# Resting tiles of 96 columns instead of 128 in the expert stage of a two-layer encoder kernel

## The reference

```
logits = (h @ router); top_v, top_i = lax.top_k(logits, 2)
top_w = softmax(top_v); comb = sum(one_hot(top_i, 8) * top_w[..., None], axis=-2)
out = 0
for e in range(8):
    out += comb[..., e:e+1] * ((silu(h @ wg[e]) * (h @ wu[e])) @ wd[e])
```

## Time and profile before

| what | us |
|---|---|
| median of 3 runs | 1901.2 |
| lowest and highest | 1900.38, 1902.32 |
| profiled execution: span from first to last instruction | 1901.2 |
| TensorE busy in it | 1863.4 (98%) |
| VectorE, ScalarE, GpSimd busy | 1442.3, 1166.7, 173.3 |

### The profile page before, as it was taken

One profiled execution on the slowest core, in us unless ns is written; L12 is line 12 of the kernel. 1 busy time (PEld: TensorE's weight loads), 2 busy tenths in 40 slices (PEclk: granted clock), 3 DMA queues, 4 the chain that ended last, 5 costly groups with the idle time before them and its releaser, 6 DMA issues.

```text
span 1901.2 us, 26671 instructions
## 1 busy us (share of the span) xinstructions
PE 1863.4 (98%) x10298; PEld 1508.3 (79%) x10298; DVE 1442.3 (76%) x1487; ACT 1166.7 (61%) x1153; POOL 173.3 (9%) x164
## 2 busy tenths in 40 slices
PE   7999999999999999999999999999999999999998
PEld 6878766788888787667888888888888888888886
DVE  4678575544546785755998989989888888898897
ACT  4575324543544663244777777777777777777776
POOL 1263003100001630031000000000000000000000
PEclk9999999999999999998999999999999999999999
DMA  9642223653556332224999999999999999999995
GB/s 313 203 156 104 90 90 133 211 193 137 199 196 214 131 131 90 90 89 146 359 361 343 367 347 358 370 341 358 365 346 365 348 356 362 341 366 347 359 367 219
DMA packets 182541, 487.79 MB, mean 257 GB/s; under 512 B 5896, under 2 KB 12676, under 8 KB 173640
## 3 DMA queue, kind: packets, MB, share of 16 engines
q1 hardware_dynamic: 177296, 477.50, 68.9%
q0 software_dynamic: 1488, 5.57, 0.9%
q10 hardware_dynamic: 3688, 3.74, 0.7%
HBM read 482.03 MB, written 1.05 MB: 254 GB/s over the span
## 4 chain that ended last, share of the span: by engine, by line
PE 88%; DVE 7%; ACT 2%; DMA 2%; issue 1%; POOL 0%; SPq 0%; DVEq 0%; ACTq 0%
PE bank L1848 48%; PE bank L1245 26%; PE bank L1458 2%; PE bank L1797 2%; PE bank L1429 1%; PE bank L1859 1%; DMA ring<-w_o_dram 1%; PE bank L1817 1%; DVE y_rwkv L1916 1%; PE bank L1237 1%; DVE ring_lo L1916 1%; DVE tmp L1916 1%; DMA h<-x_dram 1%; DVE gT_lo L1916 0%; DMA ring<-w_in_dram 0%
## 5 line engine op out<-in xcount | busy, mean ns | idle before, releaser
L1916 DVE TENSOR_TENSOR w_lo<-ring,w_hi 128x2048 fp32r<-128x2048 f32 x337 | 767.3, 2289 | 112.5 <-ACT w_hi L1147 104.1
L1147 ACT ACTIVATE w_hi<-ring 128x2048 fp32r<-128x2048 f32 x320 | 612.2, 1916 | 122.8 <-PE bank L1848 110.0
L1848 PE MATMUL bank<-w_hi,xg_hi 128*128 128x512 f32 x896 | 354.4, 396 | 1.1 <-DVE w_lo L1916 1.1
L1848 PE MATMUL bank<-w_hi,xg_lo 128*128 128x512 f32 x896 | 349.7, 390 | 0.0
L1848 PE MATMUL bank<-w_lo,xg_hi 128*128 128x512 f32 x896 | 349.5, 390 | 0.0
L1848 PEld LDWEIGHTS bank<-w_hi,xg_hi 128*128 128x128 f32 x896 | 168.8, 188 | 38.1 <-DVE w_lo L1916 4.3
L1848 PEld LDWEIGHTS bank<-w_hi,xg_lo 128*128 128x128 f32 x896 | 168.2, 188 | 35.5
L1848 PEld LDWEIGHTS bank<-w_lo,xg_hi 128*128 128x128 f32 x896 | 168.3, 188 | 33.9 <-issue 0.2
L1848 PE MATMUL bank<-w_hi,ehT_hi 128*128 128x512 f32 x448 | 176.5, 394 | 0.0
L1848 PE MATMUL bank<-w_hi,ehT_lo 128*128 128x512 f32 x448 | 174.8, 390 | 0.0
L1848 PE MATMUL bank<-w_lo,ehT_hi 128*128 128x512 f32 x448 | 174.5, 390 | 0.0
(11 more groups left out here) (434 smaller groups left out, 3036.4 us busy)
## 6 DMA issues: line engine op xcount, KB each, us to landing
ring<-moe_w_gate_dram SPq DMA_DIRECT2D x57, 2048.0 KB, 7.8
ring<-moe_w_up_dram SPq DMA_DIRECT2D x56, 2048.0 KB, 8.3
ring<-moe_w_down_dram SPq DMA_DIRECT2D x56, 2048.0 KB, 9.6
ring<-w_in_dram SPq DMA_DIRECT2D x26, 2048.0 KB, 8.1
ring<-w_branch_dram SPq DMA_DIRECT2D x6, 2048.0 KB, 8.3
ring<-ffn_w_gate_dram SPq DMA_DIRECT2D x5, 2048.0 KB, 8.1
ring<-ffn_w_up_dram SPq DMA_DIRECT2D x5, 2048.0 KB, 8.0
ring<-ffn_w_down_dram SPq DMA_DIRECT2D x5, 2048.0 KB, 8.3
```

What stands on the lines that cost most here:

```text
L1147: A.activation(w_hi[:, q % PARTS, :], ring[:, i, o:o + HALF], ACT.Copy).then_inc(s.hi_ready, 1)
L1848: ins = M(dst, a, w, start=start and n == 0, stop=stop and n == 2, skip_group_check=True)
L1916: return V.tensor_tensor(out_, a, b, op)
```

## The change

An item holds 96 slots instead of 128 (`CAP`). The resting tiles are 128 rows x 96 columns, the outputs of the large products lie on 96 partitions, an item's tokens take 96 columns of a bank; the gather streams 96 columns of `sel`; the transposes in `turn` read 96 rows of `ehm` and stream a 96x96 identity; scatter sums over 96 rows. An expert may now need up to three items and the list has room for five further ones, so `spos` and `comb` have three groups, and the list's arithmetic is written anew. The table of constants is 16 columns (64 bytes a partition) longer.

```
+CAP = 96
+GROUPS = -(-SEQ // CAP)
+MORE = (SEQ * 2 - NE) // CAP
-    c["slots"] = np.tile(np.arange(P, dtype=np.float64), (P, 1))
+    c["slots"] = np.tile(np.where(i < CAP, i, 0.5), (P, 1))
+    c["later"] = np.tile(2 * NE - np.arange(2 * NE, dtype=np.float64), (P, 1))
-    xg_hi = sb("xg_hi", [P, KD, P], F32R, where=X + 49152)
-    ehT_hi = sb("ehT_hi", [P, 28, P], F32R, where=X + 57344)
+    xg_hi = sb("xg_hi", [P, KD, CAP], F32R, where=X + 49152)
+    ehT_hi = sb("ehT_hi", [P, 28, CAP], F32R, where=X + 57344)
...
-                        ins = M(b[:, i * P:(i + 1) * P], hn[:, t, n * P:n * P + P], sel[:, t, :], start=t == 0,
+                        ins = M(b[:, i * CAP:(i + 1) * CAP], hn[:, t, n * P:n * P + P], sel[:, t, 0:CAP], start=t == 0,
...
-                        ins = M(b[:], selT[:, t * P:(t + 1) * P], part[:, 512 * u:512 * u + 512], start=i == 0,
+                        ins = M(b[:], selT[0:CAP, t * P:(t + 1) * P], part[0:CAP, 512 * u:512 * u + 512], start=i == 0,
...
-                    ins = TR(b[:, c * P:(c + 1) * P], ehm[:, j % 2, c:512:4], ident)
+                    ins = TR(b[:, c * CAP:(c + 1) * CAP], ehm[0:CAP, j % 2, c:512:4], ident[0:CAP, 0:CAP])
...
-                            ins = three(b[:], xg_hi[:, x, :], xg_lo[:, x, :], q % PARTS,
+                            ins = three(b[0:CAP, :], xg_hi[:, x, :], xg_lo[:, x, :], q % PARTS,
...
-                            ins = TR(b[:, t * P:(t + 1) * P], sel[:, t, :], ident)
+                            ins = TR(b[0:CAP, t * P:(t + 1) * P], sel[:, t, 0:CAP], ident)
...
-                            ins = three(b[:], ehT_hi[:, x, :], ehT_lo[:, x, :], q % PARTS,
+                            ins = three(b[0:CAP, :], ehT_hi[:, x, :], ehT_lo[:, x, :], q % PARTS,
...
-        for i in range(2):
-            step(V.tensor_scalar(spos[:, i, :, :], R(5), -1.0 - P * i, None, ALU.add))
+        for i in range(GROUPS):
+            step(V.tensor_scalar(spos[:, i, :, :], R(5), -1.0 - CAP * i, None, ALU.add))
-        free(V.tensor_scalar(f[:, 0:8], b[0:1, 16:24], P + 0.5, None, ALU.is_gt), "rank.1")
+        step(V.tensor_scalar(f[:, 0:8], b[0:1, 16:24], CAP + 0.5, None, ALU.is_gt))
+        free(V.tensor_scalar(f[:, 8:16], b[0:1, 16:24], 2 * CAP + 0.5, None, ALU.is_gt), "rank.1")
...
-                tt(ey_lo[:, cols], b[:], ey_hi[:, cols].bitcast(F32), ALU.subtract).then_inc(s.freed_vec, 1)
+                tt(ey_lo[0:CAP, cols], b[0:CAP, :], ey_hi[0:CAP, cols].bitcast(F32), ALU.subtract)\
+                    .then_inc(s.freed_vec, 1)
...
-                    tt(ehT_lo[:, 4 * j:4 * j + 4, :], b[:].rearrange("p (c n) -> p c n", c=4),
+                    tt(ehT_lo[:, 4 * j:4 * j + 4, :], b[:, 0:4 * CAP].rearrange("p (c n) -> p c n", c=4),
```

More of the change, by code:

```diff
@@ L480, in build @@
     rt = sb("rt", [P, 16, T, NE], where=X + 101376)
-    it_f = sb("it_f", [1, 64], where=X + 102656)
+    it_f = sb("it_f", [1, 96], where=X + 113664)
     items = sb("items", [1, 32], I32, where=X + 102912)
-    spos = sb("spos", [P, 2, T, NE], where=X + 103040)
-    comb = sb("comb", [P, 2, T, NE], where=X + 103168)
+    spos = sb("spos", [P, GROUPS, T, NE], where=X + 103040)
+    comb = sb("comb", [P, GROUPS, T, NE], where=X + 103232)
     higher = sb("higher", [P, T, NE, NE], where=X + 112640)
@@ L682, in _ @@
         sp.wait_ge(s.items_ready, 1)
-        n_items = sp.value_load(items[0:1, 24:25], min_val=SURE, max_val=SURE + 3)
+        n_items = sp.value_load(items[0:1, 26:27], min_val=SURE, max_val=SURE + MORE)
         with sp.If(n_items > SURE):
             with sp.Fori(SURE, n_items) as item:
-                e = sp.value_load(items[0:1, bass.ds(item + 12, 1)], min_val=0, max_val=NE - 1)
+                e = sp.value_load(items[0:1, bass.ds(item + NE + MORE, 1)], min_val=0, max_val=NE - 1)
                 expert_panels(e, item)
@@ L1118, in gathered_hi @@
                 for i in range(4):
-                    ins = A.activation(xg_hi[:, 4 * u + i, :], b[:, i * P:(i + 1) * P], ACT.Copy,
+                    ins = A.activation(xg_hi[:, 4 * u + i, :], b[:, i * CAP:(i + 1) * CAP], ACT.Copy,
                                        scale=gains[:, 1, 1, 4 * u + i:4 * u + i + 1])
@@ L1130, in _ @@
         act.wait_ge(s.items_ready, 1)
-        n_items = act.value_load(items[0:1, 24:25], min_val=SURE, max_val=SURE + 3)
+        n_items = act.value_load(items[0:1, 26:27], min_val=SURE, max_val=SURE + MORE)
         with act.Fori(0, n_items) as item:
@@ L1807, in _ @@
         pe.wait_ge(s.items_ready, 1)
-        n_items = pe.value_load(items[0:1, 24:25], min_val=SURE, max_val=SURE + 3)
+        n_items = pe.value_load(items[0:1, 26:27], min_val=SURE, max_val=SURE + MORE)
         def scatter(item, b_of):
@@ L2460, in _ @@
         settle()
-        step(V.tensor_scalar(selT[:], cst[:, 0:SEQ], 0.0, None, ALU.mult))
+        step(V.tensor_scalar(selT[0:CAP, :], cst[0:CAP, 0:SEQ], 0.0, None, ALU.mult))
         step(V.memset(weight[:], 0.0))
         select(0)
-        step(V.tensor_scalar(f[:, 8:16], C("experts")[0:1, :], -1.0, 8.0, ALU.mult, ALU.add))
+        more = slice(0, MORE)
+        over, first, upper = f[:, 24:32][:, more], f[:, 32:40][:, more], f[:, 40:48][:, more]
+        step(tt(f[:, 64:80], C("later")[0:1, :], f[:, 0:16], ALU.mult))
@@ L2466, in _ @@
+        step(V.reduce_sum(f[:, 56 + 26:56 + 27], f[:, 0:16], AX.X))
         settle()
-        step(tt(f[:, 8:16], f[:, 8:16], f[:, 0:8], ALU.mult))
-        step(V.reduce_sum(f[:, 56:57], f[:, 0:8], AX.X))
+        step(V.max(f[:, 16:24], f[:, 64:80]))
         settle()
-        step(V.max(f[:, 16:24], f[:, 8:16]))
+        step(V.tensor_scalar(over, f[:, 16:24][:, more], -1.0, 2.0 * NE, ALU.mult, ALU.add))
+        step(V.tensor_scalar(f[:, 82:83], f[:, 82:83], float(NE), None, ALU.add))
         settle()
-        step(V.tensor_scalar(f[:, 40:44], f[:, 16:20], -1.0, 24.0, ALU.mult, ALU.add))
@@ L2473, in _ @@
[L2473 to L2476, removed]
+        step(V.tensor_scalar(over, over, 2.0 * NE - 1, None, ALU.min))
         settle()
-        step(V.tensor_scalar(f[:, 52:56], f[:, 52:56], float(NE - 1), None, ALU.min))
-        step(V.tensor_scalar(f[:, 40:44], f[:, 40:44], float(2 * NE * T // 2 + NE - 1), None, ALU.min))
+        step(V.tensor_scalar(upper, over, NE - 0.5, float(NE), ALU.is_gt, ALU.mult))
@@ L2480, in _ @@
         settle()
-        step(V.tensor_copy(items[0:1, 0:25], f[:, 32:57]), s.items_ready)
+        step(tt(first, over, upper, ALU.add))
+        step(tt(over, over, upper, ALU.subtract))
+        settle()
+        step(V.tensor_scalar(f[:, 56 + NE:56 + NE + MORE], first, float(NE * T), None, ALU.add))
+        step(V.tensor_copy(f[:, 56 + 2 * NE + MORE:56 + 2 * NE + 2 * MORE], over))
+        step(V.tensor_copy(f[:, 56:56 + NE], C("experts")[0:1, :]))
+        step(V.tensor_copy(f[:, 56 + NE + MORE:56 + 2 * NE + MORE], C("experts")[0:1, :]))
@@ L2482, in _ @@
+        settle()
+        step(V.tensor_copy(items[0:1, 0:27], f[:, 56:83]), s.items_ready)
         dve.wait_ge(s.route_exp, 1)
@@ L2504, in gathered_lo @@
                     c = 4 * u + i
-                    ins = V.scalar_tensor_tensor(out=xg_lo[:, c, :], in0=b[:, i * P:(i + 1) * P],
+                    ins = V.scalar_tensor_tensor(out=xg_lo[:, c, :], in0=b[:, i * CAP:(i + 1) * CAP],
                                                  scalar=gains[:, 1, 1, c:c + 1], in1=xg_hi[:, c, :].bitcast(F32),
@@ L2525, in _ @@
         gathered_lo(lambda job: ahead(dve, job), 0)
-        n_items = dve.value_load(items[0:1, 24:25], min_val=SURE, max_val=SURE + 3)
+        n_items = dve.value_load(items[0:1, 26:27], min_val=SURE, max_val=SURE + MORE)
         with dve.Fori(0, n_items) as item:
-            next_column = dve.value_load(items[0:1, bass.ds(item + 1, 1)], min_val=0, max_val=NE * T + NE - 1)
+            next_column = dve.value_load(items[0:1, bass.ds(item + 1, 1)], min_val=0, max_val=NE * T * (GROUPS - 1) + NE - 1)
             def item_product(job):
```

16 lines of the change are left out of this document (8 added, 8 removed).

## The result

The changed kernel takes 1913.22 us (1912.49 to 1913.90, four runs), the kernel before 1901.43 (1900.38 to 1902.32, four runs). The ratio is 1.0068, with a 95% interval of 1.0056 to 1.0080: slower by 0.7%. The profiled execution has a span of 1910.8 us against 1901.2.

A forecast was written before the change was run, and what follows sets the result against it. TensorE's time per instruction was taken to bound the expert stage. Terms of 0 and -0.2 us summed to -0.2 us against the 1901.2 us span; likeliest time 1901.0 us, range 1887 to 1908.

The forecast's parts named there:

- second rival: Large products slow because pace depends on operand places; up to 233.4 ns each, 26 us more, 1927 us; chance 0.14.
- first rival: Large products' extra time belongs to the weight load, a quarter goes: 13.7 us less, 1887.5 us; chance 0.21.
- The large products, entered at 0: 504 an item, 4032 in all: shortening their hidden weight load changes nothing; entered 0, lower bound by the line -1.4 us.
- The gather: 32 instructions an item: the load of 128 columns sets the rate, so 0; other bound 8.0 us less.
- The turns: Seven an item: the stepped load of 128 columns sets the rate, so 0; other bound 6.6 us less.
- Scatter and the transposes of the selection: Scatter still streams 512 columns past 128 resting; the two `sel` transposes still stream 128: 0 for both.
- VectorE and ScalarE: In the loop they read a quarter fewer columns under a TensorE that doesn't wait for them: 0.
- The routing: Once: VectorE's added list operations, 0.5 to 1 us, fit into 2.74 us idle; smaller tiles after the gather save 0.1 to 0.2.
- The third: Gather and turns go with the streamed columns: 14.6 us less, 1886.6 us; chance 0.05.
- the fifth: The change runs a ninth item: 2025 us; chance 0.01.
- The fourth: Loads of 96 columns lose a fast path that 128 has: some 390 us more, 2290 us; chance 0.01.
- The limit on any gain: DMA would bind next at about 118.8 us an item, so the expert stage could give at most 40 us, 1861.

The follow-up runs named there:

- e16: Kernel before, only the large products resting on 96 columns and writing 96 partitions, step still 512 bytes; 1911.76 us against 1900.35, ratio 1.0059.
- e15: Kernel before, with padding so that streamed and resting tiles of all stages lie multiples of 256 bytes apart; 1890.41 us against 1900.35, ratio 0.9950.
- e5: Kernel before, large products reading their 128 resting columns 128 bytes behind a tile's start; 1922.16 us against 1901.03, ratio 1.0101.
- e13: Kernel before, resting tiles and all behind them moved by 128 bytes, streamed halves left in place; 1917.25 us, ratio 1.0084.
- e2: Changed kernel with tiles of 128 columns at a step of 512 bytes, list still for items of 96; 1899.75 us, ratio 0.9991.
- e1: Changed kernel, its 96-column resting tiles beginning every 512 bytes instead of every 384; 1907.11 us against 1900.42, ratio 1.0030.
- e3: Kernel before, large products reading resting tiles of 128 columns at a step of 384 bytes, overlapping; 1917.28 us against 1900.42, ratio 1.0080.
- e14: Kernel before, only the large products resting on 64 columns and writing 64 partitions; 1909.09 us against 1900.35, ratio 1.0048.
- e12: Kernel before, streamed and resting tiles of the expert stage moved together by 128 bytes; 1901.07 us, ratio 1.0003.
- e6: Changed kernel with 80 columns a tile at a step of 512 bytes; 1916.52 us against 1901.03, ratio 1.0080.

## Why the prediction was wrong

The forecast was 1901.0 us and no change, with 1887 to 1908 as the range. The measured 1913.22 lies above it, on the side of the second rival, which had a chance of 0.14: a pace that depends on where the operands lie. Its sign, more than 30.1 us for the piece of 132, came up with 30.60. That rival named one of two causes and was too large in price: I priced it with the dense part's 233.4 ns, 26 us. The piece of 132 shows 231.8 ns, and over its 504 products an item grew by 116.84 - 114.91 = 1.93 us, 15.4 us for eight. The other cause, that a narrower tile is slower by itself, stood in no rival; the first one had the width, with the opposite sign.

*The items, the bound, the load.* Right: eight items, TensorE alone in the chain before and after, and loads of 161 ns as the line between 134 and 188 gave.

*The large products, entered at 0.* This is the step that failed, in two places. The first is the sentence that shortening a hidden thing gives nothing. It was used as if it also meant that it costs nothing. e16 changes the width of the large products alone, and they take 116.02 us an item instead of 114.91; the kernel loses 0.59%. The second is the reading of the earlier trace rows. I took the extra of 20.1 ns at 512 and 10.7 ns at 256 columns for a cost that goes with the streamed columns. In both rows some distances were no multiple of 256 bytes: by the layout the streamed `f_hi` and the resting `fx_lo` lie at 96 bytes beyond a multiple of 256, the streamed `ring_lo` and the resting `fx_hi` at 128. Lined up, in e15, the extra is 227.3 - 213.3 = 14.0 ns at 512 columns and 119.9 - 106.7 = 13.2 ns at 256: nearly the same for both, as a cost per load would be. So the places added 6.1 ns at 512 columns and took 2.5 ns off at 256, and that, not the streamed columns, had made the extra seem to halve. Even so, the first rival's conclusion didn't follow: the extra is per product, and fewer resting columns made it larger, not smaller.

*The waits.* The prediction says that no row of the view of the earlier trace rows has TensorE waiting. That view was cut to its longest rows. Over the whole expert stage, from 900 to 1901 us, there is one (us in total, times, longest us):

```profile
PEld bank L1848 <- DVE w_lo L1916: 4.3, 10, 1.5
```

From 1000 to 1850 us it is 2.5 us, 0.3% of that time, so the conclusion, that TensorE's own time counts, stands.

*The second rival's evidence.* I counted it against the rival that `xg` and `ehT` lie at different places and have one pace. They do, but their places differ by multiples of 512 bytes, so they were the same place by the rule that e5 to e13 found. The evidence for it, one instruction with two paces in one trace, was the better of the two, and the two changes of address that I named (384 bytes, 64 bytes) should have been checked each for what it does to the distance between the operands. The 64 bytes moved streamed and resting tiles of the expert stage together (e2: nothing); the 384 bytes did not.

*How the loss splits.* The starts of the pieces of 132 give the length of an item: 123.80 us before, 124.92 in e16 (1249.43 to 1374.35), 124.68 in e1 (1243.85 to 1368.53), 125.55 in the changed kernel. Taken in this order, the width costs 1.12 us an item, the shorter turns and gather give 0.24 back, and the step of 384 bytes costs 0.87: 8 x (1.12 - 0.24 + 0.87) = 14.0 us. But the two causes don't add. With 128 columns the same step alone makes an item 125.79 us (e3), 1.99 over before, and its 132 products take 30.59 us where the changed kernel's take 30.60: at this step the narrower tile costs nothing more. So the loss has no split that is independent of the order.

*The gather.* Right: 3.54 us for 3.57. Streaming 96 instead of 128 columns past 128 resting ones hardly changes the pace, which fits a pace set by the load. *The turns.* Entered at 0, with 6.6 us as the other bound; they fell from 0.47 to 0.445 us, 56 x 0.025 = 1.4 us. *Scatter and the transposes of the selection.* 1.84 for 1.82 and 0.22 for 0.22.

*VectorE and ScalarE.* Right: 0.9 us less an item on VectorE, worth nothing. *The routing.* Right in that it stayed covered, and right in price: from the start of the second `sel` to the end of the small copy VectorE took 3.11 us before and 3.61 us after, 0.5 us more. The cover was less than I gave. VectorE was idle for 0.29 us ahead of the first `xg_lo`, not 2.74. The 2.74 came from the lower clock in that execution, which delayed the gather; in most of the executions with the old list, e5 for one, the same wait was 1.07 us or 1.06. So the longer list used up most of what cover there was.

```profile
890.86 0.16 DVE L2508 COPY smax<-smax 128x2 f32<-128x2 f32 x1
891.30 0.99 DVE L2516 SCALAR_TENSOR_TENSOR xg_lo<-bank,gains,xg_hi 128x96 fp32r<-128x96 f32 x4 [0.29 <-ACT xg_hi L1123]
```

*The other rivals.* The third fell with the gather, the fifth with the count of items. The fourth, the loss of a fast load, is refuted: the loads of the large products take 135 ns for 64 columns (e14), 161 for 96 and 188 for 128, about 0.83 ns a column throughout, so 128 columns have no fast path that 96 could lose. The rule of the Trainium skill that stood behind it ("TensorE: Matmul & The Clock Gate", section Weight-path perf modes), by which four-byte types gain nothing from it, agrees with that. *The limit on any gain* wasn't reached in any run.

## What to carry to other kernels

When a loop is bound by TensorE and every product has a load of its own, look at the spacing of the starts, not at the busy share, and compare it between stages: a few per cent between two stages with equal shapes pointed here at the distance between the streamed and the resting operand. Where 512 columns of this type stream, try a distance that is a multiple of 256 bytes, which costs padding alone (288 bytes a partition bought 0.5% here), and measure before narrowing a full resting tile, even where the columns removed are empty. In reading a trace, a comparison of two rows says something about one variable only if the addresses are the same too, or are known not to count.

## What the runs showed of the hardware

- The spacing of products of 512 streamed columns in the reduced float32 type, with a load of 128 columns beside each, was 226.9 ns where the two operands lay a multiple of 256 bytes apart (offsets of 0 and 256 bytes, steps of 0, 512 and 1024 bytes tried) and 233.3 ns (30.79 / 132) at offsets of 64 and of 128 bytes; with the tiles written 128 bytes further on instead of read there (e13) it was 232.3 ns. Moving both operands together changed nothing. The rows show the cost and its condition; they don't show the mechanism. That the load and the stream read at the same time and meet in the memory is a guess that fits.
- The Trainium skill ("SBUF — State Buffer", section Who interferes with whom) gives TensorE two independent read ports and names one shared pair, of VectorE and GpSimd, as the only place of contention. By that the place of one TensorE operand against the other should not count. The pair of e12 and e13 shows that it does: they differ in the place of the streamed `w_hi` and `w_lo` alone, and in time by 16 us. Here the measurement decides; whether it is the ports that meet isn't shown.
- With products of 256 columns the order was the reverse: 117.4, 118.9 and 119.9 ns for the kernel before, the one with 64 bytes more, and e15, where those of 512 columns took 233.4, 231.1 and 227.3. So the rule of 256 bytes is shown for 512 streamed columns only.
- A part of the products at an odd distance can cost as much as all of them. In the dense down projection of the kernel before, by the layout, only the streamed `ring_lo` lies 32 bytes off the resting tiles, while `f_hi` lies a multiple of 256 bytes from them, and yet the piece goes at 233.4 ns a product, against 226.9 in e15 (48.34 / 213). Which of the distances counts there isn't shown; e15 lines all of them up at once.

```profile
492.62 49.71 PE bank L1245 x213
...
488.74 48.34 PE bank L1247 x213
```

- Narrower loads of 161 ns (96 columns) and 150 (80) went with slower products than the load of 188 ns. Why, and why 72 columns change between 30.41 and 30.80 us for the same work, stays open.

The load of 80 columns, from e6's groups:

```profile
L1853 PEld LDWEIGHTS bank<-w_hi,xg_hi 128*80 128x80 f32 x896 | 134.7, 150 | 73.9 <-DVE w_lo L1921 1.6 <-issue 0.2
```
